# Rotary partners by copies, per-token key factors and one-column key sums in a two-layer transformer block, on one core

## The reference, cut to what matters

```
q = rms_norm_2(q, qh_g); k = rms_norm_2(k, kh_g)      # MLA: 8 heads of 64 + 32 rows; q too
k_rope = jnp.broadcast_to(k_rope_raw[:, :, None, :], (b, s, MLA_HEADS, MLA_ROPE))
k = jnp.concatenate([k_nope, k_rope], axis=-1)        # the 32 rotary rows are shared by all heads
q = concat([q[..., :64], apply_rope(q[..., 64:], cos, sin)])   # and k alike
q = apply_rope(rms_norm_2(q, qn_g), cos, sin)         # GQA: 8 query heads, 2 key heads of 64
k = apply_rope(rms_norm_2(k, kn_g), cos, sin)

def apply_rope(x, cos, sin):
    x1, x2 = x[..., :half], x[..., half:]
    return concat([x1 * c - x2 * s, x1 * s + x2 * c])
```

## Time and profile before

| | |
|---|---|
| median of 3 runs | 2080.78 us (2078.96 to 2081.8) |
| profiled execution, its own time | 2079.87 us |
| span of its trace | 2078.0 us, mean granted clock 0.993 |
| PE busy | 2002.1 us (96%) |
| weight loads on PE busy | 1309.6 us (63%) |
| DVE busy | 905.7 us (44%) |
| ACT busy | 641.5 us (31%) |
| the two layers | from about 1164 to 2078 us of the span |

### The profile page before, as it was taken

The page is one execution under the profiler, slowest core; times in us unless marked ns, Lnnn a source line. Parts: engine busy times, 40 slices in busy tenths (PEclk is TensorE's granted clock), DMA queues, the critical chain, the costliest instruction groups (busy, mean ns, idle before and its releaser), DMA issues.

```text
span 2078.0 us, 31430 instructions
## 1 busy us (share of the span) xinstructions
PE 2002.1 (96%) x12446; PEld 1309.6 (63%) x12447; DVE 905.7 (44%) x1591; ACT 641.5 (31%) x972; POOL 56.2 (3%) x65
## 2 busy tenths in 40 slices
PE   8999999989999999999999999999999999999999
PEld 6864333433333333333333698889999989799999
DVE  3523221212221122212212557876885549776874
ACT  1422110101111111101111344544554354635553
POOL 0000000000000000000000220000000020000000
PEclk9999999999999999999999999999999999999999
DMA  9787999479999999999999544324564644235553
GB/s 343 290 326 297 416 425 408 172 308 427 427 426 427 425 428 426 427 425 428 424 419 425 171 152 142 122 83 160 165 208 138 185 132 143 81 123 163 191 185 112
DMA packets 186466, 580.51 MB, mean 279 GB/s; under 512 B 21472, under 2 KB 138976, under 8 KB 150400
## 3 DMA queue, kind: packets, MB, share of 16 engines
q1 hardware_dynamic: 186368, 579.08, 72.0%
HBM read 577.74 MB, written 1.31 MB: 279 GB/s over the span
## 4 chain that ended last, share of the span: by engine, by line
PE 74%; DMA 18%; DVE 4%; ACT 3%; issue 2%; SPq 0%; ACTq 0%; DVEq 0%
DMA ring<-in_w_gu 16%; PE bank L1108 16%; PE bank L1116 7%; PE bank L817 4%; PE bank L1400 4%; PE bank L1640 3%; PE bank L1641 3%; PE bank L1642 3%; PE bank L1402 3%; PE bank L1401 3%; PE bank L898 2%; PE bank L1054 2%; PE bank L1068 2%; PE bank L1656 2%; PE bank L1658 1%
## 5 line engine op out<-in xcount | busy, mean ns | idle before, releaser
L1108 PE MATMUL bank<-ring,heap 128*64 128x512 f32 x2112 | 474.2, 601 | 23.3 <-DMA ring<-in_w_gu 23.3
L1108 PEld LDWEIGHTS bank<-ring,heap 128*64 128x64 f32 x2112 | 146.5, 138 | 329.2 <-issue 281.8
L2294 DVE TENSOR_SCALAR heap<-bank 128x256 f32<-128x256 f32 x66 | 24.9, 419 | 674.0 <-PE bank L1108 674.0
L1116 PE MATMUL bank<-ring,heap 128*64 128x512 f32 x1056 | 235.2, 596 | 0.0
L1793 ACT ACT_TABLE_LOAD x32 | 41.1, 1283 | 497.8 <-DVE heap L2294 497.8
L1400 PE MATMUL bank<-h_hi,w_hi 128*128 128x256 f32 x640 | 186.3, 291 | 1.2 <-DVE w_lo L2426 1.2
L2621 DVE TENSOR_TENSOR w_lo<-ring,w_hi 128x2048 fp32r<-128x2048 f32 (+1 forms) x64 | 142.4, 2225 | 100.7 <-ACT w_hi L1999 100.7
L1640 PE MATMUL bank<-h_hi,w_hi 128*128 128x256 f32 x640 | 182.4, 285 | 3.1 <-DVE w_lo L2621 3.1
L1641 PE MATMUL bank<-h_lo,w_hi 128*128 128x256 f32 x640 | 181.9, 284 | 0.0
L1642 PE MATMUL bank<-h_hi,w_lo 128*128 128x256 f32 x640 | 181.8, 284 | 0.0
L1402 PE MATMUL bank<-h_hi,w_lo 128*128 128x256 f32 x640 | 181.0, 283 | 0.0
(11 more groups left out here) (371 smaller groups left out, 3021.8 us busy)
## 6 DMA issues: line engine op xcount, KB each, us to landing
ring<-in_w_gu SPq DMA_DIRECT2D x128, 2048.0 KB, 19.0
ring<-in_w_down SPq DMA_DIRECT2D x128, 1024.0 KB, 18.1
ring<-in_ffn_w_up SPq DMA_DIRECT2D x44, 1024.0 KB, 7.7
ring<-in_w_in SPq DMA_DIRECT2D x32, 1024.0 KB, 8.4
ring<-in_w_ada SPq DMA_DIRECT2D x24, 1024.0 KB, 11.4
ring<-in_ffn_w_down SPq DMA_DIRECT2D x16, 1024.0 KB, 5.2
ring<-in_w_out SPq DMA_DIRECT2D x8, 1024.0 KB, 5.0
ring<-in_w_in SPq DMA_DIRECT2D x3, 2048.0 KB, 26.5
```

The lines of the kernel that those rows point to most:

```text
L1108: last = mm(psum[g][both[f], :], gu_input(xgT, k), wt[:, g, f, :], start=False, stop=k == DT - 1, skip_group_check=True)
L1116: last = mm(psum[bank][FEW * f:FEW * f + n, :], x[:, o:o + n], wt[:, 512 * f:512 * (f + 1)], start=k == 0, stop=k == DT - 1)
```

## The change

- **Rotary partners by copies.** The permutation matmuls and their matrices go. ACT issues DMAs inside the core's memory instead (`partners`): 2 for the shared key rows, 4 for the queries (16 partitions x 4 KB each), 8 for the grouped queries and keys (32 partitions each). DVE waits for them and multiplies in place.
- **Shared key rows turned once.** The 32 rotary rows of the key (before their norm) are scaled by the gain, turned once on 32 partitions, and copied to the eight heads by ACT.
- **Key factors per token.** The sums of the key squares come as one column per head with tokens on the partitions, as the queries' did. The root and the reciprocal are taken on 16 columns. PE then turns each column into rows (`to_rows`: transposes of a column read with stride zero), 4 for the grouped keys (`rgk`) and 16 for the eight heads (`rk0..3`), and DVE multiplies from PSUM.
- **Key squares in their own place,** so that `ga2` and the squares do not share a buffer.
- **One-column products within gate units.** 14 small products (8 for `ssgq`, 4 for `ssgk`, 2 for the shared rows) go between the steps of `ga0`; `ssq` stays in `ga2`; the 16 of `ssk` go into `ga3`.
- **New order on PE:** `sslat`, `ga0`, `ga1`, `uq`, `uk`, `uv`, `rgk`, `ga2`, `ga3`, `pl`, `ga4`, `rk0..3`, `ga5..7`, attention.

```diff
 # PE
+                gates(0, grouped_squares)
                 gates(1)
...
+                done("gstd")
+                to_rows(lay("rgk"), lambda a, t: L["rq"][:, 3, NH * t + 2 * a:NH * t + 2 * a + 1], P)
                 drained_act("uq3")
-                gates(2, query_squares)
-                done("ksq")
-                for i in range(4):
-                    squares(f"ssk{i}", const("ones")[0:MQ, 0:MQ], L["sq"], [(2 * i, 1), (2 * i + 1, 1)], MQ)
-                done("gn")
-                for i in range(2):
-                    tiles_of(lay(f"swg{i}"), const("swap_g"), L["gq"], 2 * i, P).then_inc(lay_full.sem, 1)
-                tiles_of(lay("swgk"), const("swap_g"), L["gk"], 0, P).then_inc(lay_full.sem, 1)
-                for i in range(4):
-                    tiles_of(lay(f"swq{i}"), const("swap_m")[0:MQ, 0:MQ], L["mq"], 2 * i, MQ).then_inc(lay_full.sem, 1)
+                gates(2, latent_squares("ssq", lambda i: L["sq"][:, i, :], MQ))
+                done("ksq", 2)
+                gates(3, latent_squares("ssk", lambda i: k_squares[i // 4][:, i % 4, :], HD))
...
-                for n in range(3, 7):
+                gates(4)
+                done("kstd")
+                for i in range(4):
+                    to_rows(lay(f"rk{i}"), lambda a, t: L["rq"][:, 2, NH * t + 2 * i + a:NH * t + 2 * i + a + 1], MQ)
+                for n in range(5, 8):
                     gates(n)
-                done("kn")
-                for i in range(4):
-                    tiles_of(lay(f"swk{i}"), const("swap_m")[0:MQ, 0:MQ], L["mk"], 2 * i, MQ).then_inc(lay_full.sem, 1)
-                gates(7)
 # DVE
+                own("ckv")
+                v.tensor_scalar(kr_own[64:96, :], L["krope"][64:96, :], v2("k_head", 0)[64:96], None, ALU.mult) \
+                    .then_inc(S["krope"].sem, 1)
+                c.mark(v.tensor_copy(k_gain[0:HD, :], v2("k_head", 0)[0:HD]))
+                c.mark(v.memset(k_gain[64:96, :], 1.0))
                 v.tensor_tensor(L["h"], xgain, r1.unsqueeze(1).to_broadcast([P, DT, T]), ALU.mult).then_inc(S["h1"].sem, 1)
...
-                ready("gstd")
-                scaled(L["gk"], v2("gk_head", 0), L["rs"][:, 6:8, :]).then_inc(S["gn"].sem, 1)
+                taken(scaled(L["gk"], v2("gk_head", 0), two(full("rgk"))))
                 rest_early(6)
                 taken(mean(rq[:, 0, :], full("ssq")[:, 0:2 * NH], MQ))
                 own("ssq")
                 v.reciprocal(rq[:, 0, :], rq[:, 0, :]).then_inc(S["qvar"].sem, 1)
                 rest_early(7)
...
+                taken(v.tensor_tensor(k_sums, full("ssk")[:, 0:2 * NH].rearrange("p (a b) -> p a b", a=TT),
+                                      kr_sums.unsqueeze(2).to_broadcast([P, TT, NH]), ALU.add))
+                own("ssk")
+                c.step(mean(rq[:, 2, :], rq[:, 2, :], MQ))
+                v.reciprocal(rq[:, 2, :], rq[:, 2, :]).then_inc(S["kvar"].sem, 1)
                 rest_early(8)
...
+                rest_early(9)
+                ready("swapped_q", 4 * 16)
+                by_angle(const("cos_m")[rot], mq)
+                for n in range(2):
+                    by_angle(const("sin_m")[rot], turned_at[n][rot])
+                c.settle()
+                for n in range(2):
+                    part = mq[:, 4 * n:4 * n + 4, :]
+                    v.tensor_tensor(part, part, turned_at[n][rot], ALU.add).then_inc(S["rope_m"].sem, 1)
+                ready("krows")
+                for i in range(4):
+                    k = L["mk"][0:MQ, 2 * i:2 * i + 2, :]
+                    taken(scaled(k, k_gain[0:MQ, :], two(full(f"rk{i}"))[0:MQ]))
+                rest_early(10)
+                ready("swapped_g", 8 * 16)
+                for table, x in (("sin_g", turned_g[0]), ("sin_g", turned_g[1]), ("cos_g", L["gq"]), ("cos_g", L["gk"])):
+                    by_angle(const(table), x)
                 rest_early(11)
...
 # the copies, issued by ACT
+        def partners(eng, pairs, half, first, last, done):
+            for dst, src in pairs:
+                for lo in range(first, last, 2 * half):
+                    for a, b in ((lo, lo + half), (lo + half, lo)):
+                        eng.dma_start(dst[a:a + half], src[b:b + half]).then_inc(done.sem, 16)
```

More of the change, by code:

```diff
@@ L55 @@
 STOP = None
-LCH = {"dve": 125, "pool": 23}
+LCH = {"dve": 134, "pool": 23}
 ROUNDS = 4
@@ L495, in build @@
         L["gates"] = take(24, T)
-        turned_at = [take(4, T) for _ in range(3)][0:2]
+        turned_at, third = [take(4, T) for _ in range(2)], take(4, T)
+        turned_g = L["gates"][:, 20:24, :], L["gates"][:, 14:16, :]
+        kr_own, kr_other = L["rs"][:, 6, :], L["rs"][:, 7, :]
+        k_gain = L["rq"][:, 3, NH - 1:NH]
+        k_squares = L["gates"][:, 4:8, :], third
+        kr_squares = L["rs"][:, 5, :]
+        rgk = L["rq"][:, 3, :].rearrange("p (a b) -> p a b", a=TT)[:, :, 0:4]
+        kr_sums = L["rq"][:, 3, 4:4 + TT]
         o_hi = [h_hi[:, 0:4, :], h_hi[:, 4:8, :], f_hi[:, 4:8, :]]
@@ L514, in build @@
         order += [(f"uq{i}", "act") for i in range(4)] + [(f"uk{i}", "act") for i in range(4)]
[L515 to L518, removed]
+        order += [("uv0", "act"), ("uv1", "act"), ("rgk", "dve"), ("ssq", "dve"), ("ga2", "act"), ("ssk", "dve"), ("ga3", "act")]
+        order += [("pl0", "dve"), ("pl1", "dve"), ("ga4", "act")] + [(f"rk{i}", "dve") for i in range(4)]
+        order += [(f"ga{n}", "act") for n in range(5, 8)]
         att = heads[NH:] + heads[:NH]
-        DOWN_BANKS = (3, 4, 5, 6)
+        DOWN_BANKS = (2, 3, 4, 5)
         for i in range(2 * NH + 3):
@@ L1456, in _, with by_query, grouped_squares, latent_squares @@
                 done("gsq")
-                def by_query(name, slots, rows, sums):
-                    b = lay(name)
[L1461 to L1465, removed]
+                def by_query(b, slots, rows, sums, n, j):
+                    t, i = divmod(j, slots)
+                    o = NH * t + n * i
+                    last = mm(b[:, o:o + n], rows(i)[:, P * t:P * (t + 1)], sums, start=True, stop=True)
+                    if j == TT * slots - 1:
+                        last.then_inc(lay_full.sem, 1)
+                ssgq, ssgk = lay("ssgq"), lay("ssgk")
+                by_pair = const("pair").rearrange("p (a b) -> p a b", a=2)[:, :, 0]
+                def grouped_squares(j):
+                    if j < TT:
+                        shared_squares(j)
+                    if j < 8:
+                        by_query(ssgq, 4, lambda i: L["sq"][:, 3 + i, :], by_pair, 2, j)
+                    elif j < 12:
+                        by_query(ssgk, 2, lambda i: L["gates"][:, i, :], by_pair, 2, j - 8)
+                def latent_squares(name, square, rows):
+                    b = lay(name)
+                    return lambda j: by_query(b, NH, lambda i: square(i)[0:rows, :], const("ones", 1)[0:rows, :], 1, j)
+                def shared_squares(t):
+                    mm(ssgk[:, 2 * NH + t:2 * NH + t + 1], kr_squares[64:96, P * t:P * (t + 1)], const("ones", 1)[64:96, :],
+                       start=True, stop=True)
+                gates(0, grouped_squares)
+                def to_rows(bank, column, parts):
+                    for a in range(2):
+                        for t in range(TT):
+                            last = nc.tensor.transpose(bank[0:parts, T * a + P * t:T * a + P * (t + 1)],
+                                                       column(a, t).to_broadcast([P, parts]), ident)
                     last.then_inc(lay_full.sem, 1)
-                by_query("ssgq", 4, lambda i: L["sq"][:, 3 + i, :], const("pair").rearrange("p (a b) -> p a b", a=2)[:, :, 0])
-                squares("ssgk", const("pair"), L["gates"], [(0, 1), (1, 1)])
-                gates(0)
                 gates(1)
@@ L1925, in _ @@
                 f(L["rq"][:, 1, :], L["rq"][:, 1, :], ACT.Sqrt, scale=1.0 / HD)
[L1926 removed]
+                f(rgk, rgk, ACT.Sqrt).then_inc(S["gstd"].sem, 1)
                 gates(0)
```

121 lines of the change are left out of this document (42 added, 79 removed).

## The result

The changed kernel takes 2128.95 us (median of 4 runs, 2126.97 to 2130.72) against 2080.48 for the kernel before beside it (2078.96 to 2081.8): ratio 1.0233, interval [1.0219, 1.0246], 2.3% slower. I had forecast 2092 and a range up to 2101. The direction was right; the size was wrong by 37 us, about 18.5 a layer.

The account below looks back on a forecast made before the run. PE's own instruction list bounds the stage. Per layer -8.27 of work, 9.39 of waits and 0.3 gave +2.8 us for two; with +8.5 of clock, +11.3, a median about 2092, range 2082 to 2101.

Parts of the forecast that it names:

- The work that leaves and comes: Second-layer stage on PE: 15.64 us leaves, 9.54 comes, net -6.10 a layer, -8.27 with the old waits gone.
- The transposes: On PE, for `rgk` and `rk`: 0.15 us each, 4 taking 0.59 and 16 taking 2.35.
- The waits: PE waits on DVE before `ga2` 3.07, `ga3` 2.40, `ga4` 1.07 and `ga6` 2.85: 9.39 us a layer.
- The wait before `ga4`: PE would wait 1.07 us there, since `rest_early(8)` stands behind the key factor on DVE.
- Operations on 32 partitions: DVE before `ga6`: same time as on 96 partitions for the same length; otherwise the 2.85 us wait would vanish.
- The wait of 0.3 before `h`: Ahead of the stage, three new DVE operations on shared rows delay the product making `h`: +0.3 us a layer.
- The clock: After three long waits, 3.4 us at half clock each: 5.1 us a layer, +8.5 in all less 1.7 already paid.
- My three rows of what follows a wait: In the kernel before, waits of 2.40, 1.73 and 1.53 us were each followed by 3.4 us at clock 0.50.
- Rival 3: Each wait brings two slow stretches, or the 16 transposes one too: up to six a layer, +10.2, 2102 us; chance 0.13.
- The price of a product: One-column products inside `ga0` and `ga3`: 0.22 us each, 30 of them 6.60 us a layer, price read from `ga2`.
- Costed at nothing: ACT's 14 DMA issues (0.37 us each, 5.2 a layer), the copies, weight loads, attention and bank turns: no effect.

Follow-up runs that it names:

- run 10: Run 9 with the grouped heads' turning moved on DVE from ahead of the key factor to behind `rest_early(9)`: 2062.20 us, ratio 0.9916.
- run 1: Changed kernel with one line moved: DVE makes the low half of `ga2` before scaling `gk` from `rgk`: 2105.86 us, ratio 1.0127.
- run 3: Changed kernel, waits left, with the 16 products of `ssq` behind `ga2` and those of `ssk` behind `ga3`: 2095.39 us, ratio 1.0079.
- run 4: Kernel before with one wait added: DVE waits for `uv1` before it scales `gk`, so PE waits before `ga2`: 2104.05 us, ratio 1.0120.
- run 5: Run 4 with the 16 products of `ssq` behind `ga2` instead of between its steps: 2093.16 us, ratio 1.0066.
- run 8: Run 2 with the 64-row products of `ssk` in a row behind `ga3`: 2072.95 us, ratio 0.9968.
- run 2: Changed kernel with the low parts of units 6, 7, 8 and 10 moved ahead of DVE work that waits for PE banks: 2091.35 us, ratio 1.0046.
- run 7: Run 2 with the products of `ssk` reading 96 rows, the added rows set to zero by DVE: 2069.10 us, ratio 0.9952.
- run 6: Changed kernel, waits kept, with the products of `ssk` reading 96 rows instead of 64: 2114.76 us, ratio 1.0170.
- run 9: Run 7 with the queries' and grouped heads' rotary products moved ahead of the key factor, into DVE's idle time: 2068.95 us, ratio 0.9947.

## Why the prediction was wrong, step by step

The second layer is the one I worked through, so its rows answer. Where a slow clock lies on a step, both its length and its forecast stand here.

| step | forecast us | measured us |
|---|---|---|
| `ga0`, `ga1` with 14 products | 14.76 | 15.06 |
| `uq`, `uk`, `uv` | 12.42 | 12.42 |
| `rgk` and the wait before `ga2` | 0.59 + 3.07 | 0.60 + 3.24 |
| `ga2` and the wait before `ga3` | 9.28 + 2.40 | 17.08 + 2.05 |
| `ga3` | 9.28 | 23.09 |
| `pl` and the wait before `ga4` | 1.54 + 1.07 | 2.79 + 0 |
| `ga4` | 5.84 | 5.94 |
| `rk` | 2.35 | 1.66 |
| `ga5` and the wait before `ga6` | 5.84 + 2.85 | 5.99 + 3.55 |
| `ga6`, `ga7` | 11.65 | 13.04 |
| sum | 82.94 and 5.1 of clock | 106.51 |

- **The work that leaves and comes: right.** Run 10 has all of it without waits and saves 8.92 a layer in the stage; I had 8.27. The transposes cost 0.10 each, not 0.15. The 96 columns are not the reason: in run 1, where no wait follows, the four of `rgk` with all 128 columns took 0.44 (1249.70 to 1250.14), 0.11 each. Whether it is the stride of zero or what stands behind them, the runs do not say.
- **The waits: right, in place and size.** 3.24, 2.05 and 3.55 against 3.07, 2.40 and 2.85. The wait before `ga4` is missing because `pl` ran at half clock. Operations on 32 partitions took by their length, as I had assumed: the three products by cosine and sine ended 4.6 after the first began (3.42 for two, and 1.2), where I had 4.5. The wait of 0.3 before `h` came in both layers: 0.29.
- **The clock: the step that failed.** I wrote "I count one stretch for each, 5.1 us a layer". By the table, slow clock cost `ga2` 7.8 us, `ga3` 9.3 (13.8 less the 4.5 for the rows), `pl` and `ga4` 1.4 and the last two units 1.4: 19.9 a layer. My three rows of what follows a wait were read off rightly, but behind each of those waits stood matmuls that stream 256 or 512 columns. I carried their 3.4 us to units that have a one-column product in every step. Runs 3, 4 and 5 show that this difference decides. Rival 3 had the products right and only doubled the stretches, where the trace has 44.4 us without a break; the 16 transposes that it named as well brought no fall (run 10). The Trainium skill (TensorE: Matmul & The Clock Gate, "Why this matters for your kernels"), which I weighed there, names idle gaps as what drops the clock; the trace agrees with that much, though shorter waits than it names were enough here (2.30 us before `ga6` in run 8, 2.44 before `ga3` in run 1), and what follows the wait counted for more.
- **The price of a product: right for 96 and 128 rows, wrong for 64.** "30 x 0.22" took the price in `ga2` for all. The 16 in `ga3` cost 0.50 each: 4.5 us a layer. The two 32-row products in `ga0` show it too (the first step of `ga0`, with one of them and one on 128 rows, takes 1.08, which is 0.28 over 0.36 and twice 0.22). The Trainium skill (TensorE: Matmul & The Clock Gate, "LDWEIGHTS (loading the stationary operand)") says that a load goes by its columns and not by its rows; the load records of run 2 agree, 0.30 for two loads of 96 rows and 0.29 for two of 64. What costs is that the loads of 64 rows have no head start on their product. The same page ("Step-by-step: what each phase is for") lets a load be pulled ahead when its row groups do not conflict with the running matmul or when it goes to a background buffer. Something of this kind may be the cause, but loads between 96 and 128 rows, which share row groups, have their head start in the same trace, so why those of 64 rows have none stays open.
- **Costed at nothing: right.** ACT's issues took 0.61 each by the median (0.51 to 0.89) instead of 0.37, and the copies landed in 1.8 to 7.9 us; no instruction on PE's path waited for either.

The balance: per layer the clock cost 14.8 more than forecast and the changes of rows 4.8, the waits 0.55 less and `rk` 0.7 less. That is 18.4, for two layers 36.7, of the 37 by which I was off.

Still open: why 64-row products between the steps bring the clock down by themselves in `ga3`, in some executions and not in others (run 2's spread of 20 us, against 12 us of the kernel before over all its runs); how much the products ahead of a wait have to do with a fall there, since in runs 1, 3 and 5 a unit or a row of them stood ahead of it; and why a change between 64 and 128 rows costs 0.28 where one between 96 and 128 doesn't.

## What to carry to other kernels

- A wait on PE must be priced with what stands behind it. With full-size matmuls behind the wait the clock was back after 3.4 to 6.8 us here; units with small products between their steps did not bring it back in the 17 us that one took (run 4) nor in the 42 us of two (the changed kernel). Look first for a way not to wait: here it was enough to let DVE write the next unit's weights before it waits for a bank, and that was worth 38 us with 64-row products in `ga3` (run 2 against the changed kernel) and 46 us with 96-row ones (run 7 against run 6).
- Small products between matmuls of 128 rows should have 96 rows rather than 64 or 32 where zeros can fill them: 0.22 instead of 0.50 each.
- When work is moved into an engine's idle time, follow the engine that waits for what now comes after it, as run 9 shows.

## What the runs showed of the hardware that was not expected

- The granted clock fell without any idle time: in `ga3` with 64-row products (run 2, 16.9 us), and within or at the end of a row of 16 one-column products (run 3, 6.8 and 3.4 us; run 8, 6.8 and 3.4 us; run 5, second layer, where the stretch of 6.8 us began 1 us before the wait). With 96-row products between the steps and no wait it stayed at 1.00 through both units (run 7).
- The same wait of 2.30 us before `ga6` went either way: no slow stretch in run 7, one of 3.4 us in runs 2 and 8.
- A weight load of 64 rows between matmuls of 128 rows was as long as one of 96 rows (0.29 and 0.30 us for two) but had no head start on its product (0.11 us for 96 rows), and the product cost 0.28 us more (run 2).
- Sixteen transposes of one column read with stride zero took 1.66 us, less than half of 16 one-column products (3.6).
